# Three layers of one transformer on one core: the order of GpSimd's work in attention, and of the preparation of an RWKV recurrence

## The reference, cut to what matters

```python
# attention, for each of four blocks of 128 queries
scores = einsum('bqhs,bqh->bqs', relu(q_idx @ k_idx), w_idx)      # an index of relevance
sel = top_k(causal(scores), 128)
logits = q @ k[sel] * scale + rel_bias[bucket(distance)]
probs = softmax(logits);  y_attn = probs @ v[sel]
# the recurrence's inputs
z = z + mu * (z_prev - z)                     # the shift
r, k, v, w_lo, a_lo, g_lo = split(z)
w = -softplus(-(w0 + tanh(w_lo) @ w2)) - 0.5
a = sigmoid(a0 + a_lo @ a2);  g = sigmoid(g_lo) @ g2              # low-rank products
kk = k * k_k;  kk = kk / max(norm(kk), 1e-12)                     # the key norm
k = k * (1 + (a - 1) * k_a);  decay = exp(-exp(w));  b = kk * a
# per token: state = state * decay - (state @ kk) b + v k;  y = state @ r
y_rwkv = (groupnorm(y) + sum(r * k * r_k) * v) * g
merged = sigmoid(gate_attn) * (y_attn @ Wa) + sigmoid(gate_rwkv) * (y_rwkv @ Wr)
```

## Time and profile before

| | |
|---|---|
| median of 3 runs | 3318.01 us (3315.23 to 3320.02) |
| the profiled execution | 3320.53 us, of which the span of its instructions is 3318.7 us |
| busy: PE, PEld, DVE, ACT, POOL | 3008.1, 2333.5, 1394.7, 1165.0, 1205.3 us |
| attention's 32 steps | from about 268.5 to 462.2 us of the span |
| the recurrence's preparation | from 462.2 to 536.9 us |
| granted TensorE clock, mean of the span | 0.942 |

### The profile page before, as it was taken

One profiled execution on the slowest core, in us unless ns is written; L12 is line 12 of the kernel. 1 busy time (PEld: TensorE's weight loads), 2 busy tenths in 40 slices (PEclk: granted clock), 3 DMA queues, 4 the chain that ended last, 5 costly groups with the idle time before them and its releaser, 6 DMA issues.

```text
span 3318.7 us, 40119 instructions
## 1 busy us (share of the span) xinstructions
PE 3008.1 (91%) x15600; PEld 2333.5 (70%) x15600; DVE 1394.7 (42%) x2024; ACT 1165.0 (35%) x1673; POOL 1205.3 (36%) x559
## 2 busy tenths in 40 slices
PE   7989776979999999788999999978889778999998
PEld 5856444868888886667888887746667466788886
DVE  3017537445321273422256443242277352665442
ACT  4244233244222244433342223333443523542222
POOL 3423332114444443333644444412214121544442
PEclk9998787989999999899999999978899799999999
DMA  3321110023323332224422222301112111622222
GB/s 122 101 70 64 50 47 1 3 96 108 95 95 96 102 127 75 92 76 133 163 98 95 95 95 90 114 35 62 59 48 92 45 49 47 220 95 95 95 95 83
DMA packets 80665, 284.05 MB, mean 86 GB/s; under 512 B 8968, under 2 KB 9096, under 8 KB 79744
## 3 DMA queue, kind: packets, MB, share of 16 engines
q1 hardware_dynamic: 66240, 236.36, 21.4%
q10 hardware_dynamic: 13296, 41.97, 3.3%
q0 software_dynamic: 976, 3.56, 0.3%
HBM read 260.86 MB, written 20.99 MB: 85 GB/s over the span
## 4 chain that ended last, share of the span: by engine, by line
PE 56%; issue 19%; POOL 9%; DVE 9%; ACT 5%; DMA 1%; POOLq 0%; SPq 0%; ACTq 0%; DVEq 0%
PE bank L334 15%; PE bank L336 15%; PE bank L335 15%; POOL slab_r L2702 8%; PE bank L555 2%; PE bank L441 1%; PE bank L532 1%; PE bank L609 1%; PE bank L943 1%; DVE work L2162 1%; DVE small L2160 1%; PE bank L823 1%; DVE work L2149 0%; PE bank L882 0%; PE bank L451 0%
## 5 line engine op out<-in xcount | busy, mean ns | idle before, releaser
L2702 POOL TENSOR_TENSOR slab_r<-slab,slab_high 128x1024 fp32r<-128x1024 f32 x442 | 1096.7, 2483 | 1717.8 <-ACT slab_high L1113 1717.3
L334 PE MATMUL bank<-xh,slab_high 128*128 128x512 f32 x2256 | 905.2, 401 | 39.6 <-POOL slab_r L2702 30.9
L336 PE MATMUL bank<-xh,slab_r 128*128 128x512 f32 x2256 | 887.3, 393 | 0.0
L335 PE MATMUL bank<-x_raw_r,slab_high 128*128 128x512 f32 x2064 | 813.7, 394 | 0.0
L1113 ACT CAST slab_high<-slab 128x1024 fp32r<-128x1024 f32 x442 | 462.2, 1047 | 451.3 <-DMA slab<-in_w_down 215.9
L335 PE MATMUL bank<-work_r,slab_high 128*128 128x512 f32 x1376 | 546.1, 397 | 0.0
L334 PEld LDWEIGHTS bank<-xh,slab_high 128*128 128x128 f32 x2256 | 429.9, 191 | 152.9 <-POOL slab_r L2702 34.6
L334 PE MATMUL bank<-work_r,slab_high 128*128 128x512 f32 x1184 | 474.7, 401 | 49.1 <-DVE work_r L1902 24.9
L336 PEld LDWEIGHTS bank<-xh,slab_r 128*128 128x128 f32 x2256 | 429.5, 190 | 93.5
L336 PE MATMUL bank<-work_r,slab_r 128*128 128x512 f32 x1184 | 475.8, 402 | 0.0
L335 PEld LDWEIGHTS bank<-x_raw_r,slab_high 128*128 128x128 f32 x2064 | 394.3, 191 | 80.4 <-issue 1.7
(11 more groups left out here) (465 smaller groups left out, 2860.5 us busy)
## 6 DMA issues: line engine op xcount, KB each, us to landing
slab<-in_w_down SPq DMA_DIRECT2D x88, 512.0 KB, 3.2
slab<-in_w_up SPq DMA_DIRECT2D x64, 512.0 KB, 3.2
slab<-in_w_gates SPq DMA_DIRECT2D x56, 512.0 KB, 3.3
slab<-in_w_merge SPq DMA_DIRECT2D x48, 512.0 KB, 3.8
slab<-in_w_gu SPq DMA_DIRECT2D x44, 512.0 KB, 3.5
slab<-in_w_in_a SPq DMA_DIRECT2D x32, 512.0 KB, 3.5
gates<-staging ACTq DMA_DIRECT2D x56, 256.0 KB, 2.2
slab<-in_w_out SPq DMA_DIRECT2D x24, 512.0 KB, 3.3
```

The costliest lines, as they stand in the source:

```text
L334: first = pe.matmul(bank[b][:, :], wh, mh, start=start, stop=False)
L335: pe.matmul(bank[b][:, :], wh, ml, start=False, stop=False)
L336: end = pe.matmul(bank[b][:, :], wl, mh, start=False, stop=stop)
L2702: pool.tensor_tensor(slab_low[:, slot, :], slab[:, slot, :], plain(slab_high[:, slot, :]), ALU.subtract).then_inc(S("slab_split"), 1)
```

## The change

- **Attention, GpSimd.** Step g's order becomes: bias of step g+1, shift difference of g, slab splits of g. The bias of step 0 stands ahead of the loop, and behind it the three requests for the low-rank weights, now into tiles 12 to 14, once ScalarE has copied the last index scores.
- **Attention, gates.** `IN_ATTENTION` 4 becomes 3, `AFTER_ATTENTION` 16 becomes 12: the products, high parts, splits and copies of gate tiles 12 to 15 (four slabs) go to the preparation.
- **The preparation, VectorE.** Keys times k_k come first (no wait for the low-rank results), then the four clips, then for each c: scans, the key norm's product and the other four of the round, with fewer waits for its own results. The two differences over four tiles come after the four rounds. The two four-tile products of GpSimd are made here, behind the eight operand products.
- **The preparation, TensorE.** Low-rank group 0; key sums through bank 7, each with two gate products behind it (tile 12); group 1; eight gate products (tile 13); groups 2 and 3; the bonus sums (`rk_ready`); 16 gate products (tiles 14 and 15); then the operands' waits.
- **The preparation, ScalarE.** Squares right behind the three activations; copies of groups 0 and 1; logarithms and exponentials; gate tile 12; copies of groups 2 and 3; tile 13; the decays; tiles 14 and 15.
- Tiles: keys 8 to 11, squares 48 to 51, bonus 0 to 3.

Constants:

```diff
-        IN_ATTENTION, IN_SEQUENCE, IN_MLSTM, IN_GLA, IN_LEVEL, IN_STATE = 4, 0, 6, 1, 3, 4
-        AFTER_ATTENTION = 16
+        IN_ATTENTION, IN_SEQUENCE, IN_MLSTM, IN_GLA, IN_LEVEL, IN_STATE = 3, 0, 6, 1, 3, 4
+        AFTER_ATTENTION = 12
+
+        KEYS, SQUARES, RK, LOW_RANK = 8, 48, 0, (12, 13, 14)
```

TensorE (`low_rank(c)` is the body of the old loop over c):

```diff
+            low_rank(0)
+            mark("key_sums")
             for c in range(4):
-                sum_tiles([W(28 + c)], 4 + c % 2, "dve", pair, S("kk_square"))
+                sum_tiles([W(SQUARES + c)], 7, "dve", pair, S("kk_square"))
+                early_gates(2)
+            low_rank(1)
+            early_gates(DC)
+            low_rank(2)
+            low_rank(3)
             for c in range(4):
-                sum_tiles([W(28 + c)], 4 + c, "dve", pair, S("rk_ready"))
+                sum_tiles([W(RK + c)], 4 + c, "dve", pair, S("rk_ready"))
+            early_gates(16 * DC - early[0])
```

ScalarE, after the squares:

```diff
+            low_rank(0)
+            low_rank(1)
...
             for c in range(4):
-                act.activation(W(28 + c), W(28 + c), ACT.Exp, bias=eps["kk"], scale=-0.5)\
+                act.activation(W(SQUARES + c), W(SQUARES + c), ACT.Exp, bias=eps["kk"], scale=-0.5)\
                     .then_inc(S("kk_rstd"), n.up(S("kk_rstd")))
+            send_gates(0, 13)
+            low_rank(2)
+            low_rank(3)
+            send_gates(0, 14)
...
             act.wait_ge(S("decays_ready"), n.own(S("decays_ready")))
+            send_gates(0, 16)
```

VectorE:

```diff
+            for c in range(4):
+
+                dve.wait_ge(psum_for["dve"], n.next(psum_for["dve"]))
+                dve.tensor_scalar(W(SQUARES + c), bank[7][:, :], 1e-24, 2.0 ** 30, ALU.max, ALU.mult)\
+                    .then_inc(evac, n.up(evac))
+            for c in range(4):
+                dve.wait_ge(evac_by["act"], handed_at["rwkv"]["act"] + 3 * c + 2)
...
+                dve.wait_ge(S("kk_rstd"), n.next(S("kk_rstd")))
+                dve.tensor_tensor(W(KEYS + c), W(KEYS + c), W(SQUARES + c), ALU.mult).then_inc(chain, n.up(chain))
...
+            dve.wait_ge(psum_for["dve"], n.next(psum_for["dve"], 4))
...
             dve.wait_ge(S("operands_ready"), n.own(S("operands_ready")))
+            dve.tensor_tensor(W(8, 4), W(52, 4), W(48, 4), ALU.mult).then_inc(chain, n.up(chain))
+            dve.tensor_tensor(W(12, 4), W(20, 4), W(48, 4), ALU.mult)\
+                .then_inc(S("operands_ready_2"), n.up(S("operands_ready_2")))
```

GpSimd (`biases(g)` is the old bias of step g with its waits):

```diff
+            biases(0)
+            pool.wait_ge(evac_by["act"], handed_at["attention"]["act"])
+            for i, name, rows in zip(LOW_RANK, ("w2a2", "g2a", "g2b"), (P, P, 32)):
+                pool.dma_start(W(i)[0:rows, :], a[name]).then_inc(S("lora_loads"), 16)
+            for g in range(len(steps)):
+                if g + 1 < len(steps):
+                    biases(g + 1)
...
+                gate_lows(IN_ATTENTION)
             low_parts(AFTER_ATTENTION - early[0])
...
-            pool.wait_ge(S("kb_ready"), n.next(S("kb_ready")))
-            pool.wait_ge(S("decays_ready"), n.next(S("decays_ready")))
-            pool.tensor_tensor(W(8, 4), W(52, 4), W(48, 4), ALU.mult).then_inc(chain, n.up(chain))
-            pool.tensor_tensor(W(12, 4), W(20, 4), W(48, 4), ALU.mult)\
-                .then_inc(S("operands_ready_2"), n.up(S("operands_ready_2")))
-            pool.wait_ge(S("operands_ready_2"), n.own(S("operands_ready_2")))
+            low_parts(16 - AFTER_ATTENTION)
+            early = [16] + [16 * DC] * 2
```

More of the change, by code:

```diff
@@ L653, in _, with low_rank @@
             mark("rwkv")
-            pe.wait_ge(S("lora_ready"), n.next(S("lora_ready"), 3))
-            pe.wait_ge(S("lora_loads"), n.next(S("lora_loads"), 48))
-            for c in range(4):
+            def low_rank(c):
                 s = slice(c * P, (c + 1) * P)
+                wa, g0, g1 = (W(i) for i in LOW_RANK)
                 if last[4]:
                     pe.wait_ge(*last[4])
-                pe.matmul(bank[4][:, :], W(59)[0:HD, s], W(28)[0:HD, :], start=True, stop=True)\
+                pe.matmul(bank[4][:, :], wa[0:HD, s], W(28)[0:HD, :], start=True, stop=True)\
                     .then_inc(psum_for["act"], hand(4, "act"))
@@ L2195, in _ @@
                 .then_inc(S("decay_sums"), n.up(S("decay_sums")))
[L2196 to L2219, removed]
-                    .then_inc(S("rk_ready"), n.up(S("rk_ready")))
-            dve.memset(SM(312), 0.0).then_inc(S("kb_ready"), n.up(S("kb_ready")))
-            dve.wait_ge(S("kb_ready"), n.own(S("kb_ready")))
+            dve.wait_ge(S("rk_ready"), n.own(S("rk_ready")))
+            dve.wait_ge(psum_for["dve"], n.next(psum_for["dve"], 4))
             dve.wait_ge(S("decays_ready"), n.next(S("decays_ready")))
@@ L2749, in _, with biases @@
             pool.wait_ge(evac_by["act"], handed_at["flipped"]["act"])
[L2750 to L2751 removed]
+            steps = [(i, h) for i in range(NT) for h in range(8)]
+            def biases(g):
+                i, h = steps[g]
                 w = (i + 1) * P
[L2753 removed]
+                if g == 0:
                     pool.wait_ge(S("relu_used"), n.next(S("relu_used"), 8 * (NT - 1)))
[L2755 removed]
+                elif h == 0:
                     pool.wait_ge(S("mask_ready"), n.next(S("mask_ready")))
[L2757 to L2774 removed]
@@ new lines, in biases @@
+                if g >= 2:
+                    pool.wait_ge(evac_by["dve"], handed_at["attention"]["dve"] + g - 1)
+                m = C("caus") if i == 0 else work[:, mask_at[i]:mask_at[i] + w]
+                pool.tensor_tensor(W(55 + g % 2)[:, 0:w], W(40 + h)[:, 3 * P - i * P:3 * P - i * P + w], m, ALU.add)\
+                    .then_inc(S("bias_ready"), n.up(S("bias_ready")))
+            biases(0)
+            pool.wait_ge(evac_by["act"], handed_at["attention"]["act"])
+            for i, name, rows in zip(LOW_RANK, ("w2a2", "g2a", "g2b"), (P, P, 32)):
+                pool.dma_start(W(i)[0:rows, :], a[name]).then_inc(S("lora_loads"), 16)
@@ new lines, in _ @@
+            for g in range(len(steps)):
+                if g + 1 < len(steps):
+                    biases(g + 1)
+                k = g - (SHIFT_FROM - 1)
+                if 0 <= k < len(shift_tiles):
+                    if k >= 2:
+                        pool.wait_ge(S("shift_done"), n.next(S("shift_done")))
+                    z, o = W(shift_tiles[k]), W(38 + k % 2)
+                    pool.tensor_scalar(o[:, 0:1], z[:, 0:1], -1.0, None, ALU.mult).then_inc(chain, n.up(chain))
+                    pool.tensor_tensor(o[:, 1:T], z[:, 0:T - 1], z[:, 1:T], ALU.subtract)\
+                        .then_inc(S("shift_diff"), n.up(S("shift_diff")))
+                gate_lows(IN_ATTENTION)
```

61 lines of the change are left out of this document (24 added, 37 removed).

## The result

The changed kernel takes 3283.26 us (median of four runs, 3280.71 to 3285.86), the kernel before on the same chip 3316.62. The ratio is 0.9903, 95% interval 0.9882 to 0.9925: faster by 1%, 33 us. The forecast was 3294, with a range of 3281 to 3308.

A forecast was written before the change was run, and what follows sets the result against it. The prediction took GpSimd's order, which delays the bias, to set attention's step, with the preparation one serial chain. Terms 15 + 3.5 + 9.6 - 4 = 24.1 us gave a median of 3294, range 3281 to 3308 (own range 3284 to 3305).

The forecast's parts named there:

- The loop through GpSimd: Attention: VectorE's add_max waits 39.7 us for GpSimd's bias, queued behind shift difference and split; GpSimd's order sets the step.
- the early bias would not remove the wait: Rival, attention: GpSimd comes to the bias late anyway; time 3315 us; chance 1 in 20.
- Block 2: Attention's third query block: early bias removes a 21.3 us wait, less 6 us for clock and issue, saving 15 us.
- block 2's eight steps in 41 to 46 us: Sign of being right: after the change, attention's block 2 takes 41 to 46 us for its eight steps.
- the 5 us for TensorE at its lower clock: Attention blocks 1 and 2: some long steps at the lower clock lose 1.8 us each, 5 us in all; bounds 0 to 12.
- Blocks 0 and 1: Attention's first two blocks: four steps without a round save 2.8 us, fewer splits 0.7, together 3.5 us.
- the clock eats the steps: Rival: TensorE falls to 1.2 GHz in most long steps of blocks 1 and 2; 3307 us; chance 1 in 10.
- The end of attention: Block 3's window: 60.4 us becomes 50.8 through loop waits off the path and lighter steps, saving 9.6 us.
- Weights early: Low-rank weights requested in attention: first low-rank product starts 2.3 us sooner; the requests cost 1.7 us only without cover.
- The preparation: The recurrence's preparation: new chain 71.6 us plus 7 for splits gives 78.6 against 74.7, 4 us longer.
- splits miss VectorE and the preparation takes 67 us: Rival, preparation: fully overlapped, gate products raise the clock at once; time 3282 us; chance 1 in 20.
- slower: Rival: TensorE stays at its lower clock through attention; 3378 us with all of it, about 3336 with 0.6; 3 in 100.

The follow-up runs named there:

- e1: The kernel before with only GpSimd's new order (bias one step ahead), still four gate products a step: 3286.63 us, ratio 0.9919.
- e2: The changed kernel with GpSimd's old order (bias of step g inside step g, behind the splits of g-1): 3317.63 us, ratio 1.0004.
- e7: e6 with all 16 gate tiles in attention, four products a step, so no splits in the preparation: 3282.25 us, ratio 0.9897.
- e5: The changed kernel with the last two of the four splits held back until the operands are ready: 3280.06 us, ratio 0.9894.
- e4: e5 with the two four-tile products back on GpSimd: 3284.79 us, ratio 0.9919.
- e6: e5 with all low-rank groups copied before the logarithms, and scans and decay differences ahead of VectorE's four rounds: 3275.21 us, ratio 0.9889.
- e3: The changed kernel with all 16 gate tiles in attention again, none in the preparation: 3283.07 us, ratio 0.9900.
- e9: e7 with three products a step in attention and four gate tiles among the 24 index scores ahead of it: 3293.85 us, ratio 0.9937.

## Why the prediction was right, by its steps

**As a whole.** The forecast of 3294 was 11 us too high. The measured 3283.26 lies just outside the forecast's own range, 3284 to 3305, and inside the stated 3281 to 3308, which had been widened for a rival that did not happen; that it fell there is in part luck. The mechanism held, and most of its terms were too cautious.

**The loop through GpSimd** was read rightly. The wait is gone from the earlier trace rows, e1 gives 26.5 us with nothing else changed, and e2 nothing measurable without it. The rival that the early bias would not remove the wait falls with the rows above.

**Block 2: forecast 15, measured 20.9** (58.4 us before, 37.6 after, between the starts of the same steps as in the earlier trace rows). The 21.3 us of the wait came out nearly whole. The window of the earlier trace rows holds six steps, not the eight that the prediction says, and its price of 6.2 us a step is for six. Its sign of being right, "block 2's eight steps in 41 to 46 us", therefore speaks of this window, which took 37.6; all eight took 47.3. The term that was mis-sized is the 5 us for TensorE at its lower clock. The clock did fall, as in the earlier trace rows: 0.66 in one window of 5 us of the changed kernel, 0.50 in another.

```profile
355.00:360.00 5.00, 4.99 (x17) 0.66 0.24 92
...
375.00:380.00 5.00, 5.00 (x13) 0.50 0.14 54
```

But `add_max` starts at 353.36, 360.09, 365.30 and 372.02, steps of 6.7, 5.2 and 6.7 us: the first holds the slow window and is no longer than the third, which holds none, and none is near the 8 us that I had put down for a slow step. In e7, whose clock is 1.00 from 272 to 383 us, the same steps take 6.7, 5.3 and 6.7 us, with four products each. So the lower clock cost nothing here; that TensorE works ahead of VectorE and has the slack for it is my reading.

**Blocks 0 and 1: forecast 3.5, measured 1.0** (73.9 to 72.9 us, from the first `add_max` to the start of block 2's window). The steps with rounds, which were to stay as they were, gave 2.3 in block 1. Three things took from it. The first is the weights' requests, told of below. The second is a split: the scaling of the probabilities (L2172), which TensorE's transposes wait for, takes 0.29 us alone and 2.44 beside a split that starts with it. Before, the split had begun 0.5 us sooner and the scaling took 1.99 (L2149). The step around it took 4.57 us against 4.12, and 4.56 in e7, where the clock is 1.00.

```profile
294.27 2.44 DVE L2172 TENSOR_SCALAR work<-work,small 128x128 f32<-128x128 f32 x1
294.29 2.34 POOL L2724 TENSOR_TENSOR slab_r<-slab,slab_high 128x1024 fp32r<-128x1024 f32 x1
```

The third is the clock. The last step of block 0 and the last of block 1 have no round and are TensorE's; they took 4.92 and 5.48 us, and in e5, with the same code and the clock at 1.00, 3.36 and 3.91. Here are these two steps in the changed kernel, then in e5:

```profile
298.10:303.10 5.00, 5.00 (x15) 3.29 (x16) 1.28 (x6) 1.50 (x5) 0.73 (x1) 0.66 0.00 0
336.10:341.70 5.60, 5.60 (x18) 3.86 (x19) 1.62 (x6) 1.95 (x5) 4.68 (x5) 0.70 0.00 0
...
299.10:302.60 3.50, 3.50 (x16) 2.37 (x16) 1.29 (x6) 1.50 (x5) 0.74 (x1) 1.00 0.00 0
335.60:339.60 4.00, 4.00 (x19) 2.69 (x19) 1.57 (x6) 1.89 (x5) 4.00 (x5) 1.00 0.00 0
```

That is all of the 3.1 us by which attention is shorter in e4, e5 and e6. The rival *the clock eats the steps* so happened in a small way, in other steps than it named.

**The end of attention: forecast 9.6, measured 10.7** (60.5 to 49.7 us, ten steps of 5.0). The clock stayed at 1.00 there.

**Weights early: forecast 2.3.** The first low-rank product starts 3.16 us after attention's end, against 5.46. But the cover did not hold: the bias of step 1 stands behind the three requests, and the second `add_max` waits 1.62 us for it.

```profile
269.18 0.54 POOL L2791 DMA_DIRECT2D work<-in_g2a  x1
...
269.70 0.51 POOL L2791 DMA_DIRECT2D work<-in_g2b  x1
...
270.88 0.29 DVE L2158 CUSTOM_DVE_ANT_0 work<-bank,work 128x128 f32<-128x128 f32 x1 [1.62 <-POOL work L2785]
```

From the first `add_max` to the third it is 5.0 us, against 4.3 before and 3.5 in e1, which has the new order and no requests there. So they cost 1.5 us, nearly the 1.7 that the prediction names for the case without cover, and the early weights are worth under 1 us.

**The preparation: forecast 78.6, measured 75.4,** with three terms off. The lower clock was to last 16 us and lasted to 441.7, 9.6 us after the first product: rounds began after 30.0 us instead of 33.3. The rounds with their scans were put at 17.9 and take 16.5 without the splits (e3), because each round is 3.07 us where it was 3.43, with two waits for VectorE's own results less. The splits were put at 7 of at most 9.4; all four hit, and cost 3.51 - 1.36, 2.71 - 0.75, 2.87 - 0.69 and 2.82 - 0.68: 8.4, somewhat nearer to the bound than to my choice. By the rule of the Trainium skill ("SBUF — State Buffer", section "SBUF: two separate sides") all four would be paid, and the trace agrees with 8.4 us; a scan and a product with a scalar were held up as the plain products were. The exposed exponentials were put at 6.1 and are 6.2, the operands behind them at 9.7 and are 13.9 with the two splits of 4.3 in them. Taking two products from GpSimd was to be worth 4 and is worth 4.3 (e4). The rival in which splits miss VectorE and the preparation takes 67 us did not happen, though its time, 3282, lies nearest to the measured one: attention gave what it had put down to the preparation.

**The sum.** The steps gave 20.9 + 1.0 + 10.7 - 0.7 = 31.9 us in place of 24.1. Of the 34.6 in span 2.8 are left: 0.6 less ahead of attention and 2.2 less in all that follows the first masked product. Over the ten kernels profiled here that last part varies from 2779.5 to 2786.7 us without a pattern that I could read, so I claim none of it for the change.

One more sum is wrong in the rival *slower*: its 3378 takes 250 us for TensorE's work at the lower clock and its 3336 takes 260, twice 130; with 250 the second would be 3330. Neither happened.

## What to carry to other kernels

When one engine's queue serves several consumers, ask for each of its jobs when its inputs are there and who waits for it: a bias of 1 us stood behind a wait and a job of 2.3 us that had a step of time, and putting it first was worth 26.5 us, while the lighter load beside it was worth 3 in the old order and 6 to 12 in the new one. The same question holds for what is put into the queue: three requests of half a microsecond, ahead of a bias that was due, cost 1.5 us. Work moved out of a full stage pays only what the receiving stage doesn't charge for it on any engine: the four slabs cost the preparation about 10 us as the change has them, and 5 to 6 once two of their splits waited until VectorE's operands were made. In a serial chain, what feeds another engine's long job (here the decays) goes ahead of what nobody waits for; that took the preparation from 68.1 to 61.2 us.

## What the runs showed of the hardware

Ahead of attention stand 48 small matmuls for the index scores, which no edit here but e9 touches. The same code runs at either level of TensorE's clock from one profile to the next. In the changed kernel's profile the clock is at 0.50 from 244 us to the end of the stage, though TensorE is not idle for a moment; one window of 5 us out of it:

```profile
255.00:260.00 5.00, 5.00 (x9) 0.50 0.00 0
```

In the profile of e1 it stays at 1.00, though TensorE is idle nearly a tenth of this window:

```profile
255.00:260.00 5.00, 4.60 (x17) 1.00 0.00 0
```

From the first score to the first `add_max` it is 27.7 us in the one and 20.3 in the other, 7.4 us or 0.2% of the kernel. What decides the level with which the stage runs stays open. The profiles of e1 and e2 have the full clock there, the seven others with this code the lower one; e9, with gate products between the scores, has the full clock in its one profile. In the runs of the kernel before, those at 3308.05 to 3309.4 us have a mean granted clock of 0.948 or 0.949 and those above 3314 one of 0.942 to 0.945, which fits the same two levels; two runs at 3310.2 and 3310.6 with 0.944 and 0.945 fit neither. If that reading is right, a good part of the width of the intervals is this clock. It is why an experiment of a few microseconds is read from its stage here, and not from a median.
